# Where the dilated layers of a four-layer decoder trunk scale their attention weights: GpSimd or VectorE

## The reference

```python
A_GROUPS = ((128, 1), (512, 4), (2048, 16))      # window, dilation
qkv = (h @ w_in).reshape(B, S, 3, 3, 8, 64)      # q/k/v, group, head, channel
q = rms_norm(qkv[:, :, 0], q_gain); k = rms_norm(qkv[:, :, 1], k_gain); v = qkv[:, :, 2]
# for each group:
logits = q @ k.T * 64 ** -0.5 + bias, masked to the window of its dilation
m = max(logits); p = exp(logits - m); s = sum(p)
o = (p / s) @ v
lse = m + log(s)
# over the groups:
y = sum(softmax(stack(lses)) * stack(outs)) @ w_out
```

## Time and profile before

| what | value |
|---|---|
| median of 3 runs | 2800.89 us (2800.02 to 2801.19) |
| profiled execution | 2802.51 us |
| its span, first to last instruction | 2800.7 us |
| ScalarE busy in the span | 1082.5 us (39%) |
| GpSimd busy | 1361.9 us (49%) |
| VectorE busy | 1047.0 us (37%) |
| data moved | 227.82 MB |

### The profile page before, as it was taken

One profiled execution on the slowest core, in us unless ns is written; L12 is line 12 of the kernel. 1 busy time (PEld: TensorE's weight loads), 2 busy tenths in 40 slices (PEclk: granted clock), 3 DMA queues, 4 the chain that ended last, 5 costly groups with the idle time before them and its releaser, 6 DMA issues.

```text
span 2800.7 us, 37295 instructions
## 1 busy us (share of the span) xinstructions
PE 2717.6 (97%) x14594; PEld 2191.3 (78%) x14594; DVE 1047.0 (37%) x1968; ACT 1082.5 (39%) x1640; POOL 1361.9 (49%) x1042
## 2 busy tenths in 40 slices
PE   7999999999988999999899998999999999999999
PEld 5977678888765788887788887888888977688887
DVE  4035522113495522213777774311123044622112
ACT  4355533224346433223334444422234355533221
POOL 3567444445446344445535352544545576345443
PEclk8999999999999999999999999999999999999999
DMA  4332123233422132233311110223233422132232
GB/s 126 99 83 54 46 93 103 91 105 90 104 47 69 53 104 92 90 105 91 84 46 46 46 47 30 91 91 105 92 100 86 112 54 69 48 103 91 93 102 75
DMA packets 271885, 227.82 MB, mean 81 GB/s; under 512 B 29205, under 2 KB 259349, under 8 KB 271749
## 3 DMA queue, kind: packets, MB, share of 16 engines
q1 hardware_dynamic: 260880, 216.29, 25.5%
q10 hardware_dynamic: 10868, 9.66, 1.6%
HBM read 223.62 MB, written 2.30 MB: 81 GB/s over the span
## 4 chain that ended last, share of the span: by engine, by line
PE 92%; DVE 3%; ACT 3%; issue 1%; POOL 1%; DMA 0%; ACTq 0%; DVEq 0%; POOLq 0%
PE bank L1902 50%; PE bank L1811 22%; PE bank L1968 5%; PE bank L2199 2%; PE bank L2339 1%; PE bank L1943 1%; PE bank L2025 1%; PE bank L2041 1%; PE bank L1856 1%; PE bank L2126 1%; PE bank L2005 1%; PE bank L2154 1%; POOL w_lo L580 1%; PE bank L2139 1%; PE bank L2055 1%
## 5 line engine op out<-in xcount | busy, mean ns | idle before, releaser
L580 POOL TENSOR_TENSOR w_lo<-raw,w_hi 128x512 fp32r<-128x512 f32 x808 | 1082.7, 1370 | 1089.8 <-ACT w_hi L729 1089.8
L729 ACT ACTIVATE w_hi<-raw 128x2048 fp32r<-128x2048 f32 x202 | 385.6, 1909 | 456.9 <-PE bank L1902 423.3
L1902 PE MATMUL bank<-h_hi,w_hi 128*128 128x512 f32 x1024 | 400.8, 391 | 0.0
L1902 PE MATMUL bank<-h_hi,w_lo 128*128 128x512 f32 x1024 | 398.4, 389 | 0.0
L1902 PE MATMUL bank<-h_lo,w_hi 128*128 128x512 f32 x1024 | 398.4, 389 | 0.0
L1902 PE MATMUL bank<-g_hi,w_hi 128*128 128x512 f32 x1024 | 398.3, 389 | 0.0
L1902 PE MATMUL bank<-g_lo,w_hi 128*128 128x512 f32 x1024 | 398.3, 389 | 0.0
L1902 PE MATMUL bank<-g_hi,w_lo 128*128 128x512 f32 x1024 | 398.3, 389 | 0.0
L1811 PE MATMUL bank<-h_hi,w_hi 128*128 128x512 f32 x776 | 318.0, 410 | 10.1 <-POOL w_lo L580 7.2
L1811 PE MATMUL bank<-h_lo,w_hi 128*128 128x512 f32 x776 | 310.8, 400 | 0.0
L1811 PE MATMUL bank<-h_hi,w_lo 128*128 128x512 f32 x776 | 308.4, 397 | 0.0
(11 more groups left out here) (270 smaller groups left out, 3800.4 us busy)
## 6 DMA issues: line engine op xcount, KB each, us to landing
raw<-in_mlp_w SPq DMA_DIRECT2D x128, 1024.0 KB, 5.3
raw<-in_a_w_in SPq DMA_DIRECT2D x48, 512.0 KB, 5.0
raw<-in_c_w_in SPq DMA_DIRECT2D x32, 512.0 KB, 5.4
raw<-in_a_w_in SPq DMA_DIRECT2D x12, 1024.0 KB, 5.2
raw<-in_b_w_in SPq DMA_DIRECT2D x18, 256.0 KB, 4.3
raw<-in_a_w_out SPq DMA_DIRECT2D x4, 1024.0 KB, 5.0
raw<-in_b_w_in SPq DMA_DIRECT2D x4, 1024.0 KB, 5.4
arena<-bias_scratch ACTq DMA_DIRECT2D x16, 256.0 KB, 3.7
```

Source lines behind the costliest of these rows:

```text
L580: ins = nc.gpsimd.tensor_tensor(w_lo[s][:, k, :], raw[s][:, k, :], w_hi[s][:, k, :].bitcast(F32), ALU.subtract)
L729: nc.scalar.activation(w_hi[s][:], raw[s][:], ACT.Copy).then_inc(w_hi_done, 1)
L1902: mm = nc.tensor.matmul(lin_bank[j][:], w[s][:, c, P * j:P * j + P], a[:, c, :], start=c + z == 0, stop=c == CT - 1 and z == 2)
```

## The change

GpSimd's `weights_scaled` and its call are taken out; VectorE calls its own for every unit, not for those of the last pair alone. The semaphore `an_last` and the constant `A_LAST` go, and `turn` waits on `an_done` for every unit.

```diff
--- before.py
+++ after.py
@@ -44,7 +44,6 @@
 A_NEAR, A_FAR, RW = RW_B, RW_B + 384, RW_B + 640
 A_PAIR_UNITS = 8
 A_UNITS = A_PAIR_UNITS * A_PAIRS
-A_LAST = A_UNITS - A_PAIR_UNITS
 A_FILL = 52
 A_EARLY = {26: ((0, 0, 6),), 27: ((1, 0, 6),), 29: ((0, 6, 9), (1, 6, 9))}
 A_EARLY.update({28 + j: ((j, 0, 9),) for j in range(2, CT)})
@@ -202,7 +201,6 @@
 
         as_done, al_done, ap_done, ar_done = sem("as_done"), sem("al_done"), sem("ap_done"), sem("ar_done")
         an_done, at_turned, at_copied = sem("an_done"), sem("at_turned"), sem("at_copied")
-        an_last = sem("an_last")
         apv_done, ao_done = sem("apv_done"), sem("ao_done")
         aln_done, alse_done, adelta_done = sem("aln_done"), sem("alse_done"), sem("adelta_done")
         aclamp_done, aexp_done, amix_step = sem("aclamp_done"), sem("aexp_done"), sem("amix_step")
@@ -594,17 +592,6 @@
             def mixer_a(i):
                 U0, Q = first_a[i], q_first[i]
 
-                def weights_scaled(u):
-
-                    if u >= A_LAST:
-                        return
-                    pool.wait_ge(ar_done, U0 + u + 1)
-                    for half in range(2):
-                        t = al[u % 4][:, half, 0:P * a_blocks(u)]
-                        c = 2 * (u % A_PAIR_UNITS) + half
-                        nc.gpsimd.tensor_scalar(t, t, a_stat(u // A_PAIR_UNITS, 2)[:, c:c + 1], None,
-                                                ALU.mult).then_inc(an_done, 1)
-
                 def part(G):
                     for k, n, t in a_ended(i, G - 1):
                         qk_scale(0, a_q(i, k, n, t), a_qk_tile(k, t - tile0[n]))
@@ -626,8 +613,6 @@
                         qk_scale(0, Q + 5, aq[0][5])
                     split_ahead(chunk_at["av", i, v])
                 for s in range(A_UNITS + 4):
-                    if 1 <= s <= A_UNITS:
-                        weights_scaled(s - 1)
                     share(s - 2, 6, 8)
                     share(s - 1, 2, 4)
                     part(2 * s)
@@ -1348,7 +1333,7 @@
                         t = al[u % 4][:, half, 0:P * a_blocks(u)]
                         c = 2 * (u % A_PAIR_UNITS) + half
                         nc.vector.tensor_scalar(t, t, a_stat(u // A_PAIR_UNITS, 2)[:, c:c + 1], None,
-                                                ALU.mult).then_inc(an_last, 1)
+                                                ALU.mult).then_inc(an_done, 1)
 
                 def parted(f):
 
@@ -1388,8 +1373,7 @@
                     f, z = divmod(s, A_PAIR_UNITS)
                     if 1 <= s <= A_UNITS:
                         inverses(s - 1)
-                        if s - 1 >= A_LAST:
-                            weights_scaled(s - 1)
+                        weights_scaled(s - 1)
                     if 3 <= s < A_UNITS + 3:
                         outputs(s - 3)
                     if s < A_UNITS:
@@ -2009,11 +1993,7 @@
 
                 def turn(u):
 
-                    a = first_a[i] // A_UNITS
-                    if u < A_LAST:
-                        pe.wait_ge(an_done, 2 * (A_LAST * a + u + 1))
-                    else:
-                        pe.wait_ge(an_last, 2 * (A_PAIR_UNITS * a + u - A_LAST + 1))
+                    pe.wait_ge(an_done, 2 * (U0 + u + 1))
                     if u == 0:
                         pe.wait_ge(copied, copy_first[i] + 12)
                     if U0 + u >= 2:
```

## The result

The changed kernel took 2806.29 us (median of 22 runs, 2803.07 to 2809.40), the kernel before 2801.01 us (22 runs, 2799.23 to 2803.58): 5.28 us more, a ratio of 1.0018 with a 95% interval of 1.0011 to 1.0025. The prediction said 2805.7 us, no change that a measurement could tell; with 22 runs of each kernel it can be told, since the interval lies above 1. The median of the changed kernel stands in a gap: ten of its runs lie from 2803.07 to 2804.07 us, one at 2805.47 and eleven from 2807.11 to 2809.40, so it is some 2.5 us slower in one half of its runs and some 7.5 in the other; before has no such gap.

The account below looks back on a forecast made before the run. TensorE was taken to bound the kernel (busy 2717.6 of 2800.7 us). 0.7 + 0.3 + 1.4 = 2.4 us per layer, 4.8 in two, put the median at 2805.7 us, range 2800 to 2811.

Parts of the forecast that it names:

- Unit 9: Attention loop near 201.54 us: no margin, so the scaling's delay reaches TensorE's head sums whole; 0.7 us per layer.
- Units 17 and 18: Attention loop: two GpSimd pieces and both scalings make the copy at 263.00 2.4 us late, margin 1.9; 0.3 us per layer.
- the rival in which nothing is late: Attention loops: scalings get in ahead of the pieces, shifts stay within margins; 2800 to 2802 us, chance 0.10.
- Unit 20: Attention loop near 275.11 us: GpSimd pieces hold the scaling, delaying the copy before `weigh`; 1.4 us per layer.
- the slower rival: Attention loops: closed-up pieces hold both scalings at unit 20, units 9 and 17 in full; 2807.5 us, chance 0.37.
- Seven of ten units covered: Steps where `outputs` follows at once: over 1.2 us margin and GpSimd idle in seven, so 0.61 us is covered.
- a new wait in a step called covered: Sign of being wrong: VectorE would bind in a stage where the prediction gave it room.
- Fourteen steps with cover: Attention loop steps with idle time between reciprocal and `outputs` in which the scaling fits; these cost nothing.
- pair 3: Last pair, already scaled on VectorE: unchanged, may be held a microsecond or two, with over 6 us margin; no cost.
- Faster by relief of GpSimd: Attention loops: earlier `w_lo` pieces let TensorE start tiles earlier; 2797.5 us at best, chance of over 0.2% faster 0.03.

Follow-up runs that it names:

- u9_dve: The kernel before with unit 9 of each layer alone scaled on VectorE; 2803.11 us, ratio 1.0004.
- pool_beat: The changed kernel, with GpSimd made to wait in every step until VectorE has scaled the unit; 2806.65 us, ratio 1.0017.
- after_again: The changed kernel run once more, unedited, for a second profile; 2807.95 us, ratio 1.0019 against the kernel before.
- cover14: The changed kernel with only the 14 units that have idle time behind the reciprocal scaled on VectorE, ten on GpSimd; 2801.74 us, ratio 1.0005.
- three_pool: The changed kernel with units 9, 12 and 20 of each layer back on GpSimd; 2800.41 us, ratio 0.9998.
- u20_dve: The kernel before with unit 20 of each layer alone scaled on VectorE; 2806.75 us, ratio 1.0023.

## Why the prediction was right

The forecast was 2.4 us per layer and 4.8 in all; the loops lost 2.4 to 2.8 per layer, 5.25 to 5.36 in two where the clock stayed up. The medians differ by 5.28, but that they agree so closely with the loops is in part luck: the median stands in the gap between two groups of runs, which part outside the loops, with the clock. The mechanism is the one that it named: pieces of `w_lo` close up over the scaling and hold VectorE, and what is late is what stands behind it in VectorE's queue. GpSimd at 73.5 us per loop and VectorE at 99.5 are as foreseen (71, and 90 to 110), and the mean large scaling takes 0.52 us in the loop, from this group:

```profile
L1335 DVE TENSOR_SCALAR arena<-arena 128x256 f32<-128x256 f32 x46 | 21.9, 517 | 0.8
```

Step by step:

- **Unit 9, forecast 0.7 us, measured 0.5.** The place and the path were right, and u9_dve shows it alone. The pair took 0.73 us, near the undisturbed 0.61, not a whole piece more. At 0.5 it is just under the range of 0.6 to 0.9.
- **Units 17 and 18, forecast 0.3 us (0 to 0.6), measured 0.** Unit 17 was held for 1.74 us as foreseen. But the copy at 266.10, which the trace of before has at 263.00 and which all that comes ahead of unit 17 moves by 1.6, is 1.5 us late and not 2.4, and 1.9 were margin. Unit 17's delay reached the line 1272 at 262.55 as 1.5 us and not 1.8, and there it met relief: the line took 0.69 us, where its like in the trace of before (line 1287 at 259.45) took 1.19 beside the second of the pieces of 257.57, which have moved up. Line 1365 went from 0.85 to 0.69 us without a scaling on GpSimd beside it. That these two lines get shorter the prediction had listed for the rival in which nothing is late, and left out of this sum.
- **Unit 20, forecast 1.4 us (0.5 held once, 1.8 held twice), measured 1.64.** It was held twice, which the slower rival had right. Held once, as in pool_beat, it waits 0.67. Both bounds were good to 0.2 us; the choice between them was 0.24 too low.
- **Seven of ten units covered: not unit 12.** It costs 0.46 us. This is the step that failed, and a new wait in a step called covered was among the prediction's own signs of being wrong: it assumed that GpSimd is idle by then, and checked only the scaling against the margin of over 1.2 us. The piece that moved up did not meet the scaling but line 1354 ahead of it. The rival had named unit 12, as a scaling that is held; that came in one loop of six, layer 0 of after_again, and cost 0.18 us.
- **Fourteen steps with cover, pair 3 and `turn`: nothing**, as cover14 and three_pool show.

So the sum came out near by luck as well: a term left out (0.46) and one too small (0.24) stood against two too large (0.2 and 0.3). **Faster by relief of GpSimd** is refuted: GpSimd gave up 43 us per loop and no wait of TensorE became shorter. **Nothing is late** is refuted by the waits. **Slower**, with the port lost twice, priced unit 20 rightly and came to 6.6 us because units 9 and 17 were charged in full. That two-port vector instructions and GpSimd block each other, which the prediction cited from the Trainium skill, Advanced Engine Details and Errata, VectorE Performance Modes, agrees with 2.49 us for two scalings that take 0.62 alone; that the slower rival would follow from it did not come true. The rule of the Trainium skill, GPSIMD Engine Reference, Engine selection, that elementwise work goes to VectorE did not decide the time here.

## What to carry to other kernels

What an instruction costs that is added to an in-order queue is the margin of what stands behind it, not its length: one scaling of 24 carried 3.3 of the 5.3 us lost in the loops here, and the same work put behind the copy for which TensorE waits cost next to nothing (0.2 us a loop). When work leaves an engine, look at what closes up behind it and whom that meets, on instructions that the change does not touch as well. Where whole runs spread by more than the effect, measure the stretch in which the change lies, between the same instructions.

## What the runs showed of the hardware that was not expected

The changed kernel's waits repeat within 0.3 us in three profiles, and its runs still lie in two groups some 5 us apart, which differ outside the loops and in the granted clock. Behind the same 1.64 us wait of TensorE the clock fell to 0.50 in layer 0 of one of them (283 to 285 us), and of u20_dve, and stayed at 1.00 in the two others. A short wait thus can have a second price that does not come every time: 1.6 us in layer 0 of the changed kernel, on top of 2.7. And which of two instructions gets in first where VectorE and GpSimd meet is not the same in every execution: line 1354 at unit 12 took 1.77 us in five loops of the changed kernel's three profiles and 0.68 in the sixth. The Trainium skill, TensorE: Matmul & The Clock Gate, The HAM clock gate, says of the start of a kernel that how soon the clock rises varies from run to run, and calls the loss small; here the fall and its place varied in the middle of the program as well. What decides in which execution and at which wait the clock falls stays open.
